# Memory attention of a streaming-encoder block: two heads' queries turned by VectorE instead of TensorE, and their attention placed one chunk later

## The chip, the cores and the metric

One core of a Trainium2 chip runs the whole layer in one launch. The metric is device time in microseconds (us); one execution was also profiled. TensorE (PE in the rows) multiplies, ScalarE (ACT) and VectorE (DVE) copy, split and normalise, GpSimd (POOL) does side work, SyncE (SP) issues the loads of the weights.

## The reference, cut to what matters

A residual stream of 256 tokens by 2048 passes an attention and convolution part, then attention over 256 memory tokens with 4 heads of 512, then a gated feed-forward part. All is float32. The change lies in the second part:

```python
def memory_cross_attention(h, mem_n, w_q_mem, w_kv_mem, w_o_mem):
    B, S, _ = h.shape
    q = (h @ w_q_mem).reshape(B, S, MEM_HEADS, MEM_HEAD_DIM)
    kv = (mem_n @ w_kv_mem).reshape(B, mem_n.shape[1], 2, MEM_HEADS, MEM_HEAD_DIM)
    k, v = kv[:, :, 0], kv[:, :, 1]
    s = jnp.einsum('bqhd,bmhd->bhqm', q, k).astype(jnp.float32) * MEM_HEAD_DIM ** -0.5
    p = jax.nn.softmax(s, axis=-1).astype(v.dtype)
    o = jnp.einsum('bhqm,bmhd->bqhd', p, v).reshape(B, S, D_MODEL)
    return o @ w_o_mem
```

## The kernel before, in words

Every weight matrix passes in 592 tiles of 128 by 1024 numbers through a ring of four slots. For tile g, SP loads `raw`; ScalarE rounds it to `w_hi` (`split_hi`, L809); VectorE stores the rest as `w_lo` (`split_lo`, L1311); TensorE multiplies with twelve matmuls (`products`, L365 to L367: lo by hi, hi by lo, hi by hi, for two token blocks and two rows of blocks). ScalarE may fill a slot again only once TensorE is through with the tile that lay in it, so each engine has a fixed order: at tile t of a chunk of eight, ScalarE and VectorE split tile t + 4, and side work stands between these splits. All orders are written by hand; each engine does its instructions in order, and a wait holds all that is behind it.

The stages around the change are the query projection (tiles from T_G, four chunks of eight tiles, chunk c giving the queries of head c) and the output projection (tiles from T_H, called H0, H1 and so on here). `acc` holds one chunk's result in two banks. At t = 7 ScalarE copies it to `stage` (`to_stage`, L1058) and so frees the banks for TensorE (`acc_free`).

A head h then goes these steps. In the kernel before they stand in chunk h + 1 (for head 3, in the output projection):

1. TensorE turns the queries, eight 128 by 128 transposes into `tp` (`turn_stage`, L377), after tile 0; ScalarE (L822) and VectorE (L1324) make `memqT` hi and lo of them.
2. Scores, 24 matmuls into `sc` (L701 to L703), after tile 2; VectorE takes the maxima (L1716, L1719), ScalarE the exponentials (L1190).
3. VectorE normalises (`m_norm`, L1722, L1725) at its t = 3, behind the split of that tile.
4. TensorE turns the probabilities (L711) after tile 5; ScalarE (L1196) and VectorE (L1730) make `probs_mT`.
5. Values, 24 matmuls (L724 to L726), after tile 6; ScalarE (L1200) and VectorE (L1735) make `oT`.

Keys (`key_h`, L1208 and L1741) and values (`val_h`, L1212 and L1745) of the next head are split at t = 5 and t = 6. For head 3 VectorE normalises before its split of that tile (H2), and TensorE turns the probabilities after H3. Chunks 1 to 3 are a loop on TensorE, ScalarE and VectorE.

Of the kernel before, what the change touches and what calls it, by code (L numbers as in the profile page):

```python
# [28 lines left out]
P = 128  # L29
# [21 lines left out]
HEAD_PE = {0: (0,), 2: (1,), 5: (3,), 6: (4,)}  # L51
HEAD_ACT = {0: (0,), 2: (1,), 5: (3,), 6: (4,)}
HEAD_DVE = {0: (0,), 2: (1,), 3: (2,), 5: (3,), 6: (4,)}


# [13 lines left out]
Q_K, Q_D, Q_F, Q_G, Q_H = 15, 19, 23, 24, 28  # L69

H_X, H_CQ, H_CKV, H_D, H_F, H_G, H_H = 0, 8, 10, 11, 19, 21, 29
# [17 lines left out]
def program(nc, x, memT, positions, vecs, w_in, w_uq, w_ukv, w_dwT, w_pw2, b_pw2, w_o, w_q_mem, w_kv_mem,  # L89
# [10 lines left out]
    with ctx:  # L100
# [142 lines left out]
        memv_ready = sem("memv_ready")  # L243
        m_scores, m_max0, m_max, m_exp, m_inv = (sem(n) for n in
# [101 lines left out]
        def _(pe):  # L346
# [342 lines left out]
            def mem_attention(t, h, q):  # L689
                if t == 0:  # L690
                    turn_stage(q, 2 * h + 2 * (S_G + 1))
                if t == 1:
                    operand_ready(q)
                    if not (isinstance(h, int) and h == 0):
                        pe.wait_ge(m_exp, 2 * h)
                    pe.wait_ge(key_lo, h + 1)
                    for b in range(NB):
                        for k in range(4):
                            o = sc[:, 0, b * TOK:(b + 1) * TOK]
                            hi, lo = (memqT[j][:, k, b * P:(b + 1) * P] for j in range(2))  # L700
                            mm(o, lo, key_h[0][:, k, :], start=k == 0, stop=False)  # L701
                            mm(o, hi, key_h[1][:, k, :], start=False, stop=False)
                            ins = mm(o, hi, key_h[0][:, k, :], start=False, stop=k == 3)  # L703
                    ins.then_inc(m_scores, 1)
                if t == 3:
                    pe.wait_ge(m_norm, 2 * h + 2)
                    if not (isinstance(h, int) and h == 0):
                        pe.wait_ge(m_out, h)
                    for kb in range(2):
                        for b in range(NB):  # L710
                            ins = turn(sc[:, 1, (2 * kb + b) * P:(2 * kb + b + 1) * P],  # L711
                                       probs_m[:, b, kb * P:(kb + 1) * P], ident[:, :])
                    ins.then_inc(m_turned, 1)
                if t == 4:
                    pe.wait_ge(m_out, h + 1)
                    if not (isinstance(h, int) and h == 0):
                        pe.wait_ge(o_done, 2 * h)
                    pe.wait_ge(val_lo, h + 1)
                    for g, bank in enumerate((ov, xt)):
                        for m in range(2):  # L720
                            for kb in range(2):
                                o = bank[:, m * TOK:(m + 1) * TOK]
                                at = slice((2 * g + m) * P, (2 * g + m + 1) * P)
                                mm(o, val_h[1][:, kb, at], probs_mT[0][:, kb, :], start=kb == 0, stop=False)  # L724
                                mm(o, val_h[0][:, kb, at], probs_mT[1][:, kb, :], start=False, stop=False)
                                ins = mm(o, val_h[0][:, kb, at], probs_mT[0][:, kb, :], start=False, stop=kb == 1)  # L726
                        ins.then_inc(m_pv, 1)
# [72 lines left out]
        def _(act):  # L800
# [251 lines left out]
            def to_stage(chunk, last_tile, fills, before, norm):  # L1052


                act.wait_ge(turned, before)
# [19 lines left out]
            for t in range(8):  # L1075
                if t == 7:
                    act.wait_ge(r_ready, R_MEM + 1)
                    to_stage(C_E, T_E + 8, 2 * S_K, 2 * (Q_B + 1), R_MEM)
# [5 lines left out]
            def key_chunk(c, second):  # L1084
                for t in range(8):
                    if t == 7:
                        to_stage(c + C_E, c * 8 + (T_E + 8), 2 * c + 2 * S_K, 2 * c + 2 * Q_K, R_MEM)
# [90 lines left out]
            def mem_attention(t, h, q):  # L1178
                if t == 0:
                    for g in range(2):  # L1180
                        if g == 0 and not (isinstance(h, int) and h == 0):
                            act.wait_ge(m_scores, h)
                        turned_hi_part(g, 2 * q + (g + 1), [memqT[0][:, 2 * g:2 * g + 2, :]])
                if t == 1:
                    act.wait_ge(m_max, h + 1)
                    if not (isinstance(h, int) and h == 0):
                        act.wait_ge(m_turned, h)
                        act.wait_ge(m_inv, h)
                    for b in range(NB):
                        fn(probs_m[:, b, :], sc[:, 0, b * TOK:(b + 1) * TOK], ACT.Exp, scale=MEM_SCALE,  # L1190
                           bias=negmax[:, b, 0:1], accum_out=rowsum[:, b, 0:1]).then_inc(m_exp, 1)
                if t == 3:
                    act.wait_ge(m_turned, h + 1)
                    if not (isinstance(h, int) and h == 0):
                        act.wait_ge(m_pv, 2 * h)
                    fn(probs_mT[0][:, :, :].rearrange("p k t -> p (k t)"), sc[:, 1, :], ACT.Copy).then_inc(m_out_hi, 1)  # L1196
                if t == 4:
                    for g, bank in enumerate((ov, xt)):
                        act.wait_ge(m_pv, 2 * h + (g + 1))
                        fn(oT[0][:, cols(h * 4 + 2 * g, 2), :].rearrange("p k t -> p (k t)"), bank[:, :], ACT.Copy)\  # L1200
                            .then_inc(o_hi, 1)

            def head_hi(t, h):

                if t == 5:
                    if not (isinstance(h, int) and h == 0):
                        act.wait_ge(m_scores, h)
                    fn(key_h[0][:, :, :], memKT[:, cols(h * 4, 4), :], ACT.Copy).then_inc(key_hi, 1)  # L1208
                if t == 6:
                    if not (isinstance(h, int) and h == 0):  # L1210
                        act.wait_ge(m_pv, 2 * h)
                    fn(val_h[0][:, :, :], memV[:, :, cols(h * CH, CH)], ACT.Copy).then_inc(val_hi, 1)  # L1212

            for t in range(8):
                if t == 7:
                    act.wait_ge(x_new, 4)
                    act.wait_ge(r_ready, R_CROSS + 1)
                    to_stage(C_G, T_G + 8, 2 * S_G, 2 * (Q_F + 1), R_CROSS)
                split_hi(T_G, t + 4)
                head_hi(t, 0)  # L1220
                if t == 1:
                    new_x_hi(3, crossT, "norm_cross", 2 * Q_F)
            with act.Fori(1, 4) as c:
                for t in range(8):
                    if t == 7:
                        to_stage(c + C_G, c * 8 + (T_G + 8), 2 * c + 2 * S_G, 2 * c + 2 * Q_G, R_CROSS)
                    split_hi(c * 8 + T_G, t + 4)
                    for step in HEAD_ACT.get(t, ()):
                        mem_attention(step, c - 1, c + (Q_G - 1))
                    head_hi(t, c)  # L1230


            for t in range(8):
                split_hi(T_H, t + 4)
                mem_attention(t, 3, Q_G + 3)
# [67 lines left out]
        def _(dve):  # L1303
# [402 lines left out]
            def mem_attention(t, h, q):  # L1706
                if t == 0:
                    for g in range(2):
                        if g == 0 and not (isinstance(h, int) and h == 0):
                            dve.wait_ge(m_scores, h)  # L1710
                        turned_lo_part(g, 2 * h + (H_G + g + 1), [[memqT[j][:, 2 * g:2 * g + 2, :]] for j in range(2)])
                if t == 1:
                    dve.wait_ge(m_scores, h + 1)
                    if not (isinstance(h, int) and h == 0):
                        dve.wait_ge(m_exp, 2 * h)
                    V.tensor_reduce(ssum[:, R_LN, :], sc[:, 0, :].rearrange("p (b k) -> p b k", b=NB), AX.X,  # L1716
                                    ALU.max, negate=True).then_inc(m_max0, 1)
                    dve.wait_ge(m_max0, h + 1)
# [337 lines left out]
```

## Time and profile before

| | |
|---|---|
| median of 3 runs | 1660.77 us (1660.75 to 1664.26) |
| the profiled execution's own time | 1661.55 us |
| its span, first to last instruction | 1659.7 us |
| granted TensorE clock, mean | 0.999 of full speed |
| TensorE busy | 1649.0 us, 99% of the span |
| VectorE, ScalarE, GpSimd busy | 68%, 50%, 7% |

The span is cut at the program's first and last instruction; the time of the execution lies 1.85 us above it. A row of the timeline gives start (us from the span's start), duration, engine, line, operation, output and inputs, shapes, and in brackets the idle time before it with what ended it. Matmuls are pipelined: one starts before the last one ended, so the distance from start to start is what one costs.

### The profile page before, as it was taken

What the parts mean: (1) busy time and instruction counts of PE and PEld (TensorE: products, weight loads), DVE (VectorE), ACT (ScalarE), POOL (GpSimd) and SP (SyncE); (2) the same over time, 40 slices, a digit from 0 to 9 for tenths busy, and PEclk for the clock granted to TensorE, in tenths of its full rate; (3) what the DMA queues carried; (4) which work ended last, traced back from release to release, by engine and by line L of the source; (5) the groups of instructions that cost most, each with busy time, mean ns of one, the idle gap of its engine ahead of it and who ended that gap; (6) DMA issues with size and microseconds to landing.
All of it is one profiled execution on the core that took longest, in us unless ns stands there. A gap on an engine that the chain in (4) does not pass through costs nothing.

```text
span 1659.7 us, 23379 instructions
## 1 busy us (share of the span) xinstructions
PE 1649.0 (99%) x7760; PEld 1379.9 (83%) x7760; DVE 1128.0 (68%) x1461; ACT 822.1 (50%) x1050; POOL 109.4 (7%) x154
## 2 busy tenths in 40 slices
PE   9999999999999999999999999999999999999997
PEld 8888888888888888888888888888888888888886
DVE  5678777778986466986568856666666666654453
ACT  7556545555546444566555544444444444344343
POOL 3100111120000000120001200000000000000000
PEclk9999999999999999999999999999999999999999
DMA  6875655556565665564446666666666666665564
GB/s 232 252 206 169 179 161 148 169 159 186 174 213 183 195 208 178 192 195 157 141 127 201 198 195 191 191 195 194 190 188 185 196 202 192 194 221 180 185 214 133
DMA packets 161114, 309.78 MB, mean 187 GB/s; under 512 B 10240, under 2 KB 16896, under 8 KB 160800
## 3 DMA queue, kind: packets, MB, share of 16 engines
q1 hardware_dynamic: 158864, 301.50, 59.1%
q0 software_dynamic: 1488, 6.42, 1.1%
q10 hardware_dynamic: 704, 1.11, 0.2%
q8 instruction: 34, 0.56, 0.1%
q14 instruction: 24, 0.20, 0.0%
HBM read 306.89 MB, written 2.10 MB: 186 GB/s over the span
## 4 chain that ended last, share of the span: by engine, by line
PE 97%; DMA 1%; ACT 1%; issue 1%; DVE 0%; SPq 0%; POOLq 0%; POOL 0%; ACTq 0%; DVEq 0%
PE acc L365 30%; PE acc L367 29%; PE acc L366 29%; PE tp L377 1%; DMA raw<-in_w_in_dram 1%; PE sc L518 1%; PE acc L594 1%; PE acc L596 1%; PE acc L595 1%; PE ov L499 0%; PE sc L513 0%; PE sc L488 0%; PE acc L565 0%; ACT w_hi L809 0%; PE acc L576 0%
## 5 line engine op out<-in xcount | busy, mean ns | idle before, releaser
L1311 DVE TENSOR_TENSOR w_lo<-raw,w_hi 128x1024 fp32r<-128x1024 f32 (+3 forms) x591 | 719.4, 1223 | 415.1 <-ACT w_hi L809 408.4
L809 ACT ACTIVATE w_hi<-raw 128x1024 fp32r<-128x1024 f32 (+3 forms) x591 | 605.7, 1027 | 752.8 <-PE acc L367 715.9
L365 PE MATMUL acc<-w_hi,crossT 128*128 128x512 f32 x832 | 324.8, 390 | 0.1
L366 PE MATMUL acc<-w_lo,crossT 128*128 128x512 f32 x832 | 323.9, 389 | 0.0
L367 PE MATMUL acc<-w_hi,crossT 128*128 128x512 f32 x832 | 323.8, 389 | 0.0
L365 PE MATMUL acc<-w_hi,mixT 128*128 128x512 f32 x732 | 289.3, 395 | 0.8 <-ACTq L904 0.6
L367 PE MATMUL acc<-w_hi,mixT 128*128 128x512 f32 x732 | 285.2, 390 | 0.0
L366 PE MATMUL acc<-w_lo,mixT 128*128 128x512 f32 x732 | 285.1, 389 | 0.0
L365 PEld LDWEIGHTS acc<-w_hi,crossT 128*128 128x128 f32 x832 | 156.2, 188 | 33.0 <-ACTq L1060 0.5
L367 PEld LDWEIGHTS acc<-w_hi,crossT 128*128 128x128 f32 x832 | 156.2, 188 | 32.7
L366 PEld LDWEIGHTS acc<-w_lo,crossT 128*128 128x128 f32 x832 | 156.3, 188 | 31.7
L365 PEld LDWEIGHTS acc<-w_hi,mixT 128*128 128x128 f32 x732 | 137.5, 188 | 30.1 <-DVE w_lo L1311 0.8
L367 PEld LDWEIGHTS acc<-w_hi,mixT 128*128 128x128 f32 x732 | 137.4, 188 | 29.2
L366 PEld LDWEIGHTS acc<-w_lo,mixT 128*128 128x128 f32 x732 | 137.6, 188 | 27.4
L365 PE MATMUL acc<-w_hi,actT 128*128 128x512 f32 x336 | 130.7, 389 | 0.0
L366 PE MATMUL acc<-w_lo,actT 128*128 128x512 f32 x336 | 130.7, 389 | 0.0
L367 PE MATMUL acc<-w_hi,actT 128*128 128x512 f32 x336 | 130.7, 389 | 0.0
L1443 DVE SCALAR_TENSOR_TENSOR conv<-uT,wdwT,conv (+1 forms) x240 | 119.1, 496 | 16.0 <-DVE conv L1443 12.5
L1800 DVE STREAM_TRANSPOSE row_bc<-stage 32x256 f32<-32x256 f32 x176 | 76.7, 436 | 3.6
L366 PEld LDWEIGHTS acc<-w_lo,actT 128*128 128x128 f32 x336 | 63.1, 188 | 13.2
L365 PEld LDWEIGHTS acc<-w_hi,actT 128*128 128x128 f32 x336 | 63.1, 188 | 13.0
L367 PEld LDWEIGHTS acc<-w_hi,actT 128*128 128x128 f32 x336 | 63.1, 188 | 13.0
(273 smaller groups left out, 1555.9 us busy)
## 6 DMA issues: line engine op xcount, KB each, us to landing
raw<-in_w_in_dram SPq DMA_DIRECT2D x104, 512.0 KB, 3.9
raw<-in_w_gate_dram SPq DMA_DIRECT2D x88, 512.0 KB, 4.2
raw<-in_w_up_dram SPq DMA_DIRECT2D x88, 512.0 KB, 3.7
raw<-in_w_down_dram SPq DMA_DIRECT2D x80, 512.0 KB, 4.7
raw<-in_w_kv_mem_dram SPq DMA_DIRECT2D x64, 512.0 KB, 3.8
raw<-in_w_o_dram SPq DMA_DIRECT2D x32, 512.0 KB, 4.4
raw<-in_w_q_mem_dram SPq DMA_DIRECT2D x32, 512.0 KB, 3.8
raw<-in_w_o_mem_dram SPq DMA_DIRECT2D x32, 512.0 KB, 3.8
```

Source lines behind the costliest of these rows:

```text
L365: mm(o, lo, whi, start=first and k == 0, stop=False)
L366: mm(o, hi, wlo, start=False, stop=False)
L367: ins = mm(o, hi, whi, start=False, stop=end)
L377: ins = turn(tp[:, bank, j * P:(j + 1) * P], src, ident[:, :])
L518: ins = mm(sc[:, h, at:at + keys], qnT[:, h, qs:qs + P], knT[:, h, 0:keys], start=False, stop=True, skip_group_check=True)
L594: mm(o, lo, w_hi[:, s, k * n:(k + 1) * n], start=first and k == 0, stop=False)
L595: mm(o, hi, w_lo[:, s, k * n:(k + 1) * n], start=False, stop=False)
L596: ins = mm(o, hi, w_hi[:, s, k * n:(k + 1) * n], start=False, stop=last and k == kt - 1)
L809: fn(w_hi[:, s, 0:width], raw[:, s, 0:width], ACT.Copy).then_inc(hi_done, 1)
L1311: V.tensor_tensor(w_lo[:, s, 0:width], raw[:, s, 0:width], w_hi[:, s, 0:width].bitcast(F32), ALU.subtract).then_inc(lo_done, 1)
L1443: ins = V.scalar_tensor_tensor(out=a, in0=u, scalar=wt, in1=a, op0=ALU.mult, op1=ALU.add)
L1800: ins = V.transpose(dst[:, :, :, 32 * i:32 * i + 32], src[:, :, :, 32 * j:32 * j + 32])
```

## The change

- The queries of heads 0 and 1 are no longer turned by TensorE. VectorE turns them in squares of 32 by 32, sixteen instructions per head from `stage` to the buffer `x_f[0]`, spread over t = 0 to 5 of chunks 1 and 2 as 3, 3, 3, 3, 2, 2; ScalarE and VectorE then make `memqT` from it at t = 6, with one instruction of 128 by 1024 each. The new semaphores are `mq_turned`, `mq_hi` and `mq_lo`.
- The attention of heads 0 and 1 moves a chunk later: scores after tile 1, probabilities after tile 4, values after tile 5 of chunks 2 and 3.
- Head 2 is still turned by TensorE, after tile 0 of chunk 3; its scores come after tile 4 there, its probabilities after tile 7, its values after tile H0.
- Head 3 keeps its places on TensorE; VectorE normalises it after the split at H2 and no longer before it.
- The splits of keys and values move with their heads. The loop over chunks 1 to 3 is written out on all three engines.

```diff
-            with pe.Fori(1, 4) as c:
+            for c in range(1, 4):
                 for t in range(8):
                     products(c * 8 + T_G, t, 8, crossT, 2 * t, 2, CH, c + C_G)
-                    for step in HEAD_PE.get(t, ()):
-                        mem_attention(step, c - 1, c + (Q_G - 1))
+                    if c == 3 and t == 0:
+                        mem_queries(2)
+                    if c > 1 and t == 1:
+                        mem_scores(c - 2)
+                    if c > 1 and t == 4:
+                        mem_probs_turn(c - 2)
+                        if c == 3:
+                            mem_scores(2)
+                    if c > 1 and t == 5:
+                        mem_values(c - 2)
+                    if c == 3 and t == 7:
+                        mem_probs_turn(2)
...
+                if t == 0:
+                    mem_queries(3)
+                    mem_values(2)
+                if t == 1:
+                    mem_scores(3)
+                if t == 3:
+                    mem_probs_turn(3)
+                if t == 4:
+                    mem_values(3)
...
+            def mem_queries_hi(h):
+
+                if h > 0:
+                    act.wait_ge(m_scores, h)
+                if h < 2:
+                    act.wait_ge(mq_turned, h + 1)
+                    fn(memqT[0][:, :, :], x_f[0], ACT.Copy).then_inc(mq_hi, 1)
...
-            with act.Fori(1, 4) as c:
+            for c in range(1, 4):
                 for t in range(8):
                     if t == 7:
-                        to_stage(c + C_G, c * 8 + (T_G + 8), 2 * c + 2 * S_G, 2 * c + 2 * Q_G, R_CROSS)
+                        to_stage(c + C_G, c * 8 + (T_G + 8), 2 * c + 2 * S_G,
+                                 *((mq_turned, c) if c < 3 else (turned, 2 * (Q_G + 1))), R_CROSS)
                     split_hi(c * 8 + T_G, t + 4)
...
+                    if c == 3 and t == 1:
+                        mem_exp(1)
+                        mem_queries_hi(2)
+                    if c == 2 and t == 1:
+                        mem_exp(0)
+                    if c > 1 and t == 2:
+                        keys_hi(c - 1)
+                    if c > 1 and t == 4:
+                        mem_probs_hi(c - 2)
+                        if c == 3:
+                            mem_exp(2)
+                    if c > 1 and t == 5:
+                        mem_out_hi(c - 2)
+                    if c < 3 and t == 6:
+                        mem_queries_hi(c - 1)
...
+            def mem_query_turns(t, h):
+
                 if t == 0:
+                    dve.wait_ge(stage_full, 2 * (S_G + h + 1))
+                    dve.wait_ge(x_lo_out, 3)
+                    if h > 0:
+                        dve.wait_ge(mq_lo, h)
+                for n in range((0, 3, 6, 9, 12, 14, 16, 16)[t], (3, 6, 9, 12, 14, 16, 16, 16)[t]):
+                    i, j = n // 4, n % 4
+                    src = stage[32 * i:32 * i + 32, :, :].rearrange("p b (k c) -> p b k c", c=P)
+                    dst = x_f[0][32 * j:32 * j + 32, :, :].rearrange("p k (b t) -> p b k t", b=NB)
+                    ins = V.transpose(dst[:, :, :, 32 * i:32 * i + 32], src[:, :, :, 32 * j:32 * j + 32])
+                if t == 5:
+                    ins.then_inc(mq_turned, 1)
...
-            with dve.Fori(1, 4) as c:
+            for c in range(1, 4):
                 for t in range(8):
                     split_lo(c * 8 + T_G, t + 4)
...
+                    if c == 3 and t == 1:
+                        mem_max(1)
+                        mem_queries_lo(2)
+                    if c == 2 and t == 1:
+                        mem_max(0)
+                    if c > 1 and t == 2:
+                        keys_lo(c - 1)
+                    if c > 1 and t == 3:
+                        mem_norm(c - 2)
+                    if c > 1 and t == 4:
+                        mem_probs_lo(c - 2)
+                        if c == 3:
+                            mem_max(2)
+                    if c < 3:
+                        mem_query_turns(t, c - 1)
+                    if c > 1 and t == 5:
+                        mem_out_lo(c - 2)
+                        if c == 3:
+                            mem_norm(2)
+                            values_lo(2)
+                    if c < 3 and t == 6:
+                        mem_queries_lo(c - 1)
...
+                if t == 0:
+                    mem_probs_lo(2)
+                    mem_queries_lo(3)
                 split_lo(T_H, t + 4)
-                if t not in (0, 2):
-                    mem_attention(t, 3, Q_G + 3)
...
+                if t == 2:
+                    mem_norm(3)
+                    values_lo(3)
```

## Rows read from the trace of the kernel before

**Rows 1.** The page: busy time of TensorE, share of the span, instructions.
```profile
PE 1649.0 (99%) x7760; PEld 1379.9 (83%) x7760; DVE 1128.0 (68%) x1461; ACT 822.1 (50%) x1050; POOL 109.4 (7%) x154
```
**Rows 2.** Timeline, chunk 1, the turn of head 0's queries among the matmuls.
```profile
752.76 0.39 PE L367 MATMUL acc<-w_hi,crossT 128*128 128x512 f32 x1
...
752.99 1.03 PE L377 MATMUL tp<-ident,stage 128*128 128x128 f32 x8
...
753.78 0.48 PE L365 MATMUL acc<-w_hi,crossT 128*128 128x512 f32 x1
...
754.10 0.40 PE L366 MATMUL acc<-w_lo,crossT 128*128 128x512 f32 x1
```
**Rows 3.** Timeline, the border from chunk 0 to chunk 1.
```profile
748.42 1.04 ACT L1212 ACTIVATE val_h<-memV 128x1024 fp32r<-128x1024 f32 x1
...
749.37 1.48 ACT L1058 ACTIVATE stage<-acc,rfac 128x512 f32<-128x512 f32 x2
749.46 0.39 PE L366 MATMUL acc<-w_lo,crossT 128*128 128x512 f32 x1
...
749.69 0.39 PE L367 MATMUL acc<-w_hi,crossT 128*128 128x512 f32 x1
...
750.13 0.19 PEld L365 LDWEIGHTS acc<-w_hi,crossT 128*128 128x128 f32 x1 [0.48 <-ACTq L1060]
750.14 0.50 PE L365 MATMUL acc<-w_hi,crossT 128*128 128x512 f32 x1
...
750.47 0.40 PE L366 MATMUL acc<-w_lo,crossT 128*128 128x512 f32 x1
```
**Rows 4.** Timeline, chunk 1, from the end of head 0's scores to its probabilities.
```profile
762.19 0.40 PE L365 MATMUL acc<-w_hi,crossT 128*128 128x512 f32 x1
...
763.12 0.17 DVE L1719 TENSOR_SCALAR negmax<-ssum 128x2 f32<-128x2 f32 x1
...
764.15 0.20 ACT L1190 ACTIVATION_READ_ACCUMULATOR probs_m<-sc,negmax 128x1 f32 x1
...
765.14 1.06 ACT L809 ACTIVATE w_hi<-raw 128x1024 fp32r<-128x1024 f32 x1 [0.79 <-PE acc L367]
...
766.23 1.23 DVE L1311 TENSOR_TENSOR w_lo<-raw,w_hi 128x1024 fp32r<-128x1024 f32 x1 [2.95 <-ACT w_hi L809]
...
767.38 0.16 DVE L1722 RECIPROCAL rowinv<-rowsum 128x2 f32<-128x2 f32 x1
...
767.57 0.62 DVE L1725 TENSOR_SCALAR probs_m<-probs_m,rowinv 128x256 f32<-128x256 f32 x2
767.66 0.39 PE L365 MATMUL acc<-w_hi,crossT 128*128 128x512 f32 x1
...
770.39 0.60 PE L711 MATMUL sc<-ident,probs_m 128*128 128x128 f32 x4
```
**Rows 5.** Timeline of VectorE, squares turned and splits close behind each other.
```profile
693.55 1.33 DVE L1670 STREAM_TRANSPOSE row_bc<-stage 32x256 f32<-32x256 f32 x3
694.90 1.23 DVE L1311 TENSOR_TENSOR w_lo<-raw,w_hi 128x1024 fp32r<-128x1024 f32 x1
```
**Rows 6.** Groups by form, VectorE, 655 to 860 us: squares; split of keys.
```profile
L1670 DVE STREAM_TRANSPOSE x_f<-stage 32x256 f32<-32x256 f32 x32 | 13.9, 435 | 0.6
...
L1741 DVE TENSOR_TENSOR row_r<-memKT,row_r 128x1024 fp32r<-128x1024 f32 x4 | 4.9, 1217 | 0.0
```
**Rows 7.** Groups by form, ScalarE, 727 to 860 us: table loads.
```profile
L809 ACT ACT_TABLE_LOAD x3 | 3.8, 1283 | 0.1
```
**Rows 8.** Timeline of ScalarE, a table load and what follows it.
```profile
37.20 1.28 ACT L891 ACT_TABLE_LOAD   x1
38.49 0.31 ACT L891 ACTIVATE trig<-resid 128x128 f32<-128x128 f32 x1
```
**Rows 9.** Timeline, output projection: head 3's normalising, the split at H2, its probabilities.
```profile
848.92 0.62 DVE L1725 TENSOR_SCALAR probs_m<-probs_m,rowinv 128x256 f32<-128x256 f32 x2
...
850.63 1.23 DVE L1311 TENSOR_TENSOR w_lo<-raw,w_hi 128x1024 fp32r<-128x1024 f32 x1 [1.09 <-ACT w_hi L809]
...
852.01 0.60 PE L711 MATMUL sc<-ident,probs_m 128*128 128x128 f32 x4
```
**Rows 10.** The page, DMA issues: KB each, median us from issue to landing.
```profile
raw<-in_w_q_mem_dram SPq DMA_DIRECT2D x32, 512.0 KB, 3.8
```

More of the change, by code:

```diff
@@ L686, in _ @@
                 x_update(c, T_F, C_F, mixT)
[L689 to L696, printed above, removed]
-                    for b in range(NB):
[L698 to L727, printed above, removed]
@@ new lines, in mem_queries, with mem_scores @@
+            def mem_queries(h):
+                turn_stage(Q_G + h - 2, 2 * (S_G + h + 1))
+            def mem_scores(h):
+                if h < 2:
+                    pe.wait_ge(mq_lo, h + 1)
+                else:
+                    operand_ready(Q_G + h - 2)
+                if h > 0:
+                    pe.wait_ge(m_exp, 2 * h)
+                pe.wait_ge(key_lo, h + 1)
+                for b in range(NB):
+                    for k in range(4):
+                        o = sc[:, 0, b * TOK:(b + 1) * TOK]
+                        hi, lo = (memqT[j][:, k, b * P:(b + 1) * P] for j in range(2))
+                        mm(o, lo, key_h[0][:, k, :], start=k == 0, stop=False)
+                        mm(o, hi, key_h[1][:, k, :], start=False, stop=False)
+                        ins = mm(o, hi, key_h[0][:, k, :], start=False, stop=k == 3)
+                ins.then_inc(m_scores, 1)
@@ new lines, in mem_probs_turn, with mem_values @@
+            def mem_probs_turn(h):
+                pe.wait_ge(m_norm, 2 * h + 2)
+                if h > 0:
+                    pe.wait_ge(m_out, h)
+                for kb in range(2):
+                    for b in range(NB):
+                        ins = turn(sc[:, 1, (2 * kb + b) * P:(2 * kb + b + 1) * P],
+                                   probs_m[:, b, kb * P:(kb + 1) * P], ident[:, :])
+                ins.then_inc(m_turned, 1)
+            def mem_values(h):
+                pe.wait_ge(m_out, h + 1)
+                if h > 0:
+                    pe.wait_ge(o_done, 2 * h)
+                pe.wait_ge(val_lo, h + 1)
+                for g, bank in enumerate((ov, xt)):
+                    for m in range(2):
+                        for kb in range(2):
+                            o = bank[:, m * TOK:(m + 1) * TOK]
+                            at = slice((2 * g + m) * P, (2 * g + m + 1) * P)
+                            mm(o, val_h[1][:, kb, at], probs_mT[0][:, kb, :], start=kb == 0, stop=False)
+                            mm(o, val_h[0][:, kb, at], probs_mT[1][:, kb, :], start=False, stop=False)
+                            ins = mm(o, val_h[0][:, kb, at], probs_mT[0][:, kb, :], start=False, stop=kb == 1)
+                    ins.then_inc(m_pv, 1)
@@ L1049, in _, with to_stage @@
             gate_and_pair(PAIRS - 1, PAIRS - 1, 1, last=True)
-            def to_stage(chunk, last_tile, fills, before, norm):
-                act.wait_ge(turned, before)
+            def to_stage(chunk, last_tile, fills, read, before, norm):
+                act.wait_ge(read, before)
                 for b in range(NB):
@@ L1175, in _ @@
                 x_update(c, T_F, 0, S_F, Z_F, R_CROSS, "norm_cross")
-            def mem_attention(t, h, q):
-                if t == 0:
-                    for g in range(2):
[L1181 to L1212, printed above, removed]
+            def mem_queries_hi(h):
+                if h > 0:
+                    act.wait_ge(m_scores, h)
+                if h < 2:
+                    act.wait_ge(mq_turned, h + 1)
+                    fn(memqT[0][:, :, :], x_f[0], ACT.Copy).then_inc(mq_hi, 1)
+                else:
+                    for g in range(2):
+                        turned_hi_part(g, 2 * (Q_G + h - 2) + (g + 1), [memqT[0][:, 2 * g:2 * g + 2, :]])
@@ new lines, in mem_exp, with mem_probs_hi @@
+            def mem_exp(h):
+                act.wait_ge(m_max, h + 1)
+                if h > 0:
+                    act.wait_ge(m_turned, h)
+                    act.wait_ge(m_inv, h)
+                for b in range(NB):
+                    fn(probs_m[:, b, :], sc[:, 0, b * TOK:(b + 1) * TOK], ACT.Exp, scale=MEM_SCALE,
+                       bias=negmax[:, b, 0:1], accum_out=rowsum[:, b, 0:1]).then_inc(m_exp, 1)
+            def mem_probs_hi(h):
+                act.wait_ge(m_turned, h + 1)
+                if h > 0:
+                    act.wait_ge(m_pv, 2 * h)
+                fn(probs_mT[0][:, :, :].rearrange("p k t -> p (k t)"), sc[:, 1, :], ACT.Copy).then_inc(m_out_hi, 1)
@@ new lines, in mem_out_hi, with keys_hi @@
+            def mem_out_hi(h):
+                for g, bank in enumerate((ov, xt)):
+                    act.wait_ge(m_pv, 2 * h + (g + 1))
+                    fn(oT[0][:, h * 4 + 2 * g:h * 4 + 2 * g + 2, :].rearrange("p k t -> p (k t)"), bank[:, :], ACT.Copy)\
+                        .then_inc(o_hi, 1)
+            def keys_hi(h):
+                if h > 0:
+                    act.wait_ge(m_scores, h)
+                fn(key_h[0][:, :, :], memKT[:, h * 4:h * 4 + 4, :], ACT.Copy).then_inc(key_hi, 1)
@@ L1214, in _, with values_hi @@
+            def values_hi(h):
+                if h > 0:
+                    act.wait_ge(m_pv, 2 * h)
+                fn(val_h[0][:, :, :], memV[:, :, h * CH:(h + 1) * CH], ACT.Copy).then_inc(val_hi, 1)
             for t in range(8):
@@ L1233, in _ @@
+                    if c < 3 and t == 6:
+                        mem_queries_hi(c - 1)
+                    if c == 3 and t == 6:
+                        keys_hi(3)
+                    if c == 2 and t == 7:
+                        values_hi(1)
+                    if c == 3 and t == 5:
+                        values_hi(2)
             for t in range(8):
+                if t == 0:
+                    mem_probs_hi(2)
                 split_hi(T_H, t + 4)
-                mem_attention(t, 3, Q_G + 3)
+                if t == 0:
+                    mem_queries_hi(3)
+                    mem_out_hi(2)
@@ L1236, in _ @@
+                if t == 1:
+                    mem_exp(3)
+                if t == 2:
+                    values_hi(3)
+                if t == 3:
+                    mem_probs_hi(3)
+                if t == 4:
+                    mem_out_hi(3)
                 if t == 7:
@@ new lines, in mem_query_turns, with mem_queries_lo @@
+                if t == 5:
+                    ins.then_inc(mq_turned, 1)
+            def mem_queries_lo(h):
+                if h < 2:
+                    dve.wait_ge(mq_hi, h + 1)
+                    V.tensor_tensor(memqT[1][:, :, :], x_f[0], memqT[0][:, :, :].bitcast(F32), ALU.subtract)\
+                        .then_inc(mq_lo, 1)
+                else:
+                    dve.wait_ge(m_scores, h)
+                    for g in range(2):
+                        turned_lo_part(g, 2 * (h - 2) + (H_G + g + 1), [[memqT[j][:, 2 * g:2 * g + 2, :]] for j in range(2)])
@@ new lines, in mem_max, with mem_norm @@
+            def mem_max(h):
+                dve.wait_ge(m_scores, h + 1)
+                if h > 0:
+                    dve.wait_ge(m_exp, 2 * h)
+                V.tensor_reduce(ssum[:, R_LN, :], sc[:, 0, :].rearrange("p (b k) -> p b k", b=NB), AX.X,
+                                ALU.max, negate=True).then_inc(m_max0, 1)
+                dve.wait_ge(m_max0, h + 1)
+                V.tensor_scalar(negmax[:, :, 0], ssum[:, R_LN, :], MEM_SCALE, None, ALU.mult).then_inc(m_max, 1)
+            def mem_norm(h):
+                dve.wait_ge(m_exp, 2 * h + 2)
+                V.reciprocal(rowinv[:, :, 0], rowsum[:, :, 0]).then_inc(m_inv, 1)
+                dve.wait_ge(m_inv, h + 1)
+                for b in range(NB):
+                    V.tensor_scalar(probs_m[:, b, :], probs_m[:, b, :], rowinv[:, b, 0:1], None, ALU.mult)\
+                        .then_inc(m_norm, 1)
@@ new lines, in mem_probs_lo, with mem_out_lo @@
+            def mem_probs_lo(h):
+                dve.wait_ge(m_out_hi, h + 1)
+                hi, lo = (probs_mT[j][:, :, :].rearrange("p k t -> p (k t)") for j in range(2))
+                V.tensor_tensor(lo, sc[:, 1, :], hi.bitcast(F32), ALU.subtract).then_inc(m_out, 1)
+            def mem_out_lo(h):
+                for g, bank in enumerate((ov, xt)):
+                    dve.wait_ge(o_hi, 2 * h + (g + 1))
+                    hi, lo = (oT[j][:, h * 4 + 2 * g:h * 4 + 2 * g + 2, :].rearrange("p k t -> p (k t)") for j in range(2))
+                    V.tensor_tensor(lo, bank[:, :], hi.bitcast(F32), ALU.subtract).then_inc(o_done, 1)
@@ new lines, in keys_lo, with values_lo @@
+            def keys_lo(h):
+                dve.wait_ge(key_hi, h + 1)
+                V.tensor_tensor(key_h[1][:, :, :], memKT[:, h * 4:h * 4 + 4, :], key_h[0][:, :, :].bitcast(F32),
+                                ALU.subtract).then_inc(key_lo, 1)
+            def values_lo(h):
+                dve.wait_ge(val_hi, h + 1)
+                V.tensor_tensor(val_h[1][:, :, :], memV[:, :, h * CH:(h + 1) * CH], val_h[0][:, :, :].bitcast(F32),
+                                ALU.subtract).then_inc(val_lo, 1)
```

86 lines of the change are left out of this document (29 added, 57 removed).

## The prediction, made before the changed kernel was run

> **What bounds the kernel now.** I read the page first: TensorE is busy for 99% of the span and runs at full clock [rows 1]. So only two things move the time: work taken from or given to TensorE, and moments in which it waits. I then read the timeline of the stage that the change touches, once for TensorE (where is the distance from one matmul's start to the next more than usual?) and once for VectorE and ScalarE (how long before TensorE needs it is each result ready?). Usual is 0.23 us for 512 columns: 749.46 to 749.69 [rows 3]. A tile of twelve is 2.72 us: two tiles lie between 762.19 and 767.66 [rows 4]. From the start of chunk 1 to the end of the output projection's first chunk, some 116 us, I find one wait over 0.1 us: 0.22 us at the border of chunks 0 and 1 [rows 3]. The reader is to see that in this stage nearly every side result is early, and that how early it is, is what the change spends.
>
> **Taken from TensorE: two turns of queries.** Without a turn the second matmul after the one at 752.76 would start 0.45 us later, at 753.21; it starts at 754.10 [rows 2]. A turn group of eight so costs 0.88 us, and two cost 1.76. Scores, probabilities and values are the same number of matmuls at other places: nothing.
>
> **Given to VectorE: 32 squares.** One takes 0.435 us [rows 6], three with a split behind them 1.34 [rows 5], thus 0.447 each and 7.15 per head. A tile has 2.72 us, a split takes 1.15 of it (766.23 to 767.38 [rows 4]). In chunk 1 three squares and a split are 2.49 us, which fits; nothing else is in VectorE's way there. The two final instructions of 128 by 1024 take the place of four of 128 by 512, on engines with time to spare. The Trainium skill (VectorE: DVE Perf Modes, Rules for kernel authors) would give a full 128 by 128 transpose to TensorE if PSUM will do as its destination; that is against this change, and by rows 2 and 5 it is right about cost (0.88 us against 7.15), but the change buys TensorE's time with VectorE's. It alters no term.
>
> **Wait 1: head 0's probabilities, in chunk 2.** Here VectorE has the squares of head 1 and the attention of head 0 together, and TensorE now turns the probabilities after tile 4, three tiles after the scores, where before it had three tiles as well but VectorE had nothing more to do. I set zero at the first matmul behind the scores (762.19 [rows 4]) and write down VectorE's queue from the same rows. Maxima end at 1.10 (763.29). The squares of t = 1 end at 2.44, under cover: the split of t = 2 can't begin before 4.04 (766.23), since it waits for TensorE's tile and for ScalarE. Then all is queue: split 1.15, keys 1.14 (1.217 less the overlap that a split shows), three squares 1.34, split of t = 3 1.15, normalising 0.81 (767.38 to 768.19). Sum 4.04 + 5.59 = 9.63, and 0.09 to reach TensorE (the copy of rows 3 ends about 750.05, TensorE goes on at 750.14). TensorE is there after three tiles, at 8.16. It waits 1.56 us.
>
> **A table load on top.** Before, ScalarE loads a function table at the top of each of the three passes of the loop [rows 7], far from anything urgent. Written out, one load is left, and I expect it directly in front of the first user, as at 37.20 [rows 8], which here is the exponential of head 0. There it costs 1.28 + 0.02 us. The exponentials end at 2.16 (764.35 [rows 4]) without it and at 3.46 with it; ScalarE's next split would begin at 2.95 (765.14). It begins 0.5 us late, the queue above has no slack behind it, and wait 1 becomes 2.06. If the load stays early or overlaps the wait for the maxima, this term is 0. The Trainium skill (ScalarE: Activation LUTs, What ACT_TABLE_LOAD costs) counts a drain of 1.38 us to every such load, 2.66 us in all; the trace has the next instruction 1.29 us after the start of the load [rows 8], so the rows show no such drain. By the rule wait 1 would be about 3.4 us.
>
> **Waits 2 and 3: normalising behind a split, one tile before its use.** Head 1 in chunk 3: VectorE's t = 3 is split, then normalising; TensorE wants it after tile 4. In the kernel before the same pair ended at 768.19, and TensorE ended the tile in question at 767.66 [rows 4]; it was not late only because the turn stood one tile further on, at 770.39. So now 768.19 + 0.09 - 767.66 = 0.62 us. Head 3: normalising was through at 849.54, before the split of H2; behind that split it ends at 850.63 + 1.15 + 0.81 = 852.59, with 0.09 for the signal 852.68, against 852.01 [rows 9]: 0.67 us. Head 2 has two tiles for it, so nothing.
>
> **Waits 4 and 5: the borders of chunks 1 to 2 and 2 to 3.** ScalarE's t = 6 is now a split and a copy of 128 by 1024 (`mem_queries_hi`) with no values between TensorE's tiles 6 and 7. That is the picture of rows 3, where `val_h` delays the emptying of `acc`: TensorE goes on at 750.14 where 749.92 was due, and the matmul after it is 0.33 behind instead of 0.23, a restart of 0.11. So 0.33 us each, 0.66. At the old two borders the values gave ScalarE time. At the border to the output projection the turn of head 2's probabilities gives it.
>
> **Priced at nothing.** The ring: a split is done 2.3 us after its slot came free (765.1 to 767.4 [rows 4]) and used three tiles, 8.2 us, after that slot came free, so 5.9 us are cover, of which the queue spends up to 2. The transfer for a slot (3.8 us [rows 10]) is issued when that split is done and is wanted when TensorE is through with the slot, 8.2 + 2.7 - 2.3 = 8.6 us later; 2 us less still cover it. Head 2's values after H0: behind tile 7 ScalarE has half of the copy to `stage` (0.74 [rows 3]), a split (0.97) and a copy of 512 columns (at most 0.74), VectorE one of 512 (at most 0.75, being half the size of a split of 1.15 with its fixed part), 3.2 us and some signals; TensorE has H0 and a turn in front of it, 3.6, and the turn of the probabilities before them. The moved splits of keys and values have a tile or more, but for the keys counted above. If the ring's cover were gone, each late microsecond would be one of TensorE's. The loop written out: branches show no gap on TensorE before; between 0 and the largest unexplained gap at a stage's edge, 0.1 us per chunk, I take 0.
>
> **Sum.** -1.76 + 1.56 + 0.50 + 0.62 + 0.67 + 0.66 = +2.25 us. Without the table term +1.75; with a restart of 0.11 after each of the three long waits +2.6. Against the profiled execution's 1661.55 that gives 1663.8; its time is 0.8 above the median of the runs, and I carry the difference to the median: 1660.77 + 2.25 = 1663.0. A measurement of this kernel can tell about 0.2%, 3.3 us, from no change: my forecast is no change that can be told.
>
> **Rivals.** A, all is covered: VectorE's queue is shorter than I write it (squares overlap with splits more, the normalising is early), the waits vanish and the turns are gained: -1.76, 1659.0. For it: the stage has hardly a wait now. Against: waits 2 and 3 need no load at all, they follow from order. Chance 0.10, with the cases between it and mine. B, the other side, slower by over 3.3 us: VectorE's queue in chunk 2 is longer, and wait 1 decides it. It needs 1.1 us more than in my sum, for instance 0.12 us more on each of the nine instructions in the queue, or a table load that holds ScalarE as long as the rule above says (there +3.6 us). Doubling wait 1 gives +4.3, 1665.1. For it: the queue has no slack, so all of it counts. Against: each duration has a row. Chance 0.14. C, writing out the loop costs instruction fetching: bounded by the parts written out before, where I find no gaps; three engines at 0.3 us per chunk would give +0.9, 1663.9. Chance 0.06, nearly all within the bound. Mine has 0.70, with 1661.8 to 1664.2 as its own range.
>
> **The range.** From 1659.5, which takes in A with half a microsecond of waits left, to 1665.3, just past B's doubled wait. Faster by over 0.2% would need -3.3 us, twice what is taken from TensorE; only the spread of the runs could show it: 0.03. Slower is B: 0.14. Same is the rest: 0.83.
>
> **What would show it.** In the changed profile: 16 transposes fewer on TensorE; VectorE gapless from the split of t = 2 to the squares of t = 3 in chunk 2; TensorE idle about 2 us before head 0's probabilities, 0.6 before those of heads 1 and 3, 0.2 at two borders; one table load in the stage, in front of head 0's exponential. Wrong would be: probabilities without a wait (A), one of over 3 us or TensorE waiting for `w_lo` (B), even thinning of matmuls (C).

## The result, and the profile after

| | before | after |
|---|---|---|
| median | 1661.20 us (20 runs) | 1663.72 us (20 runs) |
| profiled execution | 1661.55 us | 1663.47 us |
| its span | 1659.7 us | 1661.6 us |

The ratio is 1.0014, 95% interval 1.0007 to 1.0020. The changed kernel is 2.5 us slower; the interval, 1.2 to 3.3 us, leaves no doubt that it is slower, and little about the size. The forecast was +2.25 us, and no change that can be told from the spread of the times.

For differences this small the traces are sharper than the times. I take the length of the two stages that hold the change, from the first matmul of the query projection to the first of the feed-forward part, and call it the stage: 727.17 to 931.96 us before, 204.79 us; 726.75 to 933.56 us after, 206.81 us. It grew by 2.02 us. The rest of the span differs by -0.1 us net.

The page after, with the busy times, is to be read beside [rows 1]:

```profile
PE 1647.8 (99%) x7744; PEld 1378.0 (83%) x7744; DVE 1140.8 (69%) x1491; ACT 819.8 (49%) x1046; POOL 107.9 (6%) x154
```

TensorE has 16 instructions fewer and 1.2 us less of work, and yet the span is longer. So it waits, and the waits view of TensorE names for whom (us in total, times, longest; a wait is counted only from when nothing else of TensorE was in flight):

```profile
PE sc L714 <- DVE probs_m L1816: 2.5, 3, 1.5
...
PE acc L361 <- ACTq L1083: 0.5, 3, 0.2
```

Three waits for normalised probabilities, three at borders of chunks. The longest, in chunk 2, in the timelines of TensorE, VectorE and ScalarE; it is to be read beside [rows 4]:

```profile
780.47 0.40 PE L361 MATMUL acc<-w_hi,crossT 128*128 128x512 f32 x1
...
788.43 0.39 PE L363 MATMUL acc<-w_hi,crossT 128*128 128x512 f32 x1
790.32 0.55 PE L714 MATMUL sc<-ident,probs_m 128*128 128x128 f32 x3 [1.50 <-DVE probs_m L1816]
```
```profile
784.57 1.23 DVE L1379 TENSOR_TENSOR w_lo<-raw,w_hi 128x1024 fp32r<-128x1024 f32 x1 [1.64 <-ACT w_hi L832]
785.71 1.22 DVE L1835 TENSOR_TENSOR row_r<-memKT,row_r 128x1024 fp32r<-128x1024 f32 x1
786.96 1.33 DVE L1785 STREAM_TRANSPOSE x_f<-stage 32x256 f32<-32x256 f32 x3
788.31 1.23 DVE L1379 TENSOR_TENSOR w_lo<-raw,w_hi 128x1024 fp32r<-128x1024 f32 x1
789.45 0.16 DVE L1813 RECIPROCAL rowinv<-rowsum 128x2 f32<-128x2 f32 x1
789.64 0.62 DVE L1816 TENSOR_SCALAR probs_m<-probs_m,rowinv 128x256 f32<-128x256 f32 x2
```
```profile
778.93 1.28 ACT L1219 ACT_TABLE_LOAD   x1
781.60 0.48 ACT L1219 ACTIVATE probs_m<-sc,negmax 128x256 f32<-128x256 f32 x1 [1.38 <-DVE negmax L1808]
```

From 784.57 on VectorE has no idle time: split, keys, three squares, split, normalising, in this order. TensorE would have gone on at 788.66 (one matmul's 0.23 after 788.43) and goes on at 790.32: 1.66 us. The table load stands in front of the first exponential, but it runs at 778.93, while ScalarE has to wait for the maxima anyway, and is over at 780.21.

The wait before head 1's probabilities, and the border of chunks 1 and 2, to be read beside [rows 3]:

```profile
819.56 0.39 PE L363 MATMUL acc<-w_hi,crossT 128*128 128x512 f32 x1
820.43 0.66 PE L714 MATMUL sc<-ident,probs_m 128*128 128x128 f32 x4 [0.48 <-DVE probs_m L1816]
```
```profile
771.50 0.39 PE L363 MATMUL acc<-w_hi,crossT 128*128 128x512 f32 x1
772.04 0.47 PE L361 MATMUL acc<-w_hi,crossT 128*128 128x512 f32 x1 [0.15 <-ACTq L1083]
772.34 0.39 PE L362 MATMUL acc<-w_lo,crossT 128*128 128x512 f32 x1
```

Start to start is 0.87 instead of 0.23 in the first: 0.64 us lost. Head 3's (852.81 to 853.68) is the same. At the border 0.54 instead of 0.23, and 0.30 behind it: 0.39 us. The border of chunks 2 and 3 loses 0.39 too, and the old one, of chunks 0 and 1, now also 0.39 where it was 0.33. The sum is -1.76 + 1.66 + 2 x 0.64 + 2 x 0.39 + 0.06 = 2.02 us, all of the stage's growth. That it fits to the last digit is chance: other distances differ by up to 0.1 us between the two traces and cancel.

### The profile page after: what moved, and what is told of

The parts are those of the page before. It is cut to its first block, busy times and chain, and to the rows that moved or that the text cites. A ratio compares the mean times of both kernels' runs of the same rounds, so it can differ in the third digit from the quotient of the medians.

```text
span 1661.6 us, 23215 instructions
## 1 busy us (share of the span) xinstructions
PE 1647.8 (99%) x7744; PEld 1378.0 (83%) x7744; DVE 1140.8 (69%) x1491; ACT 819.8 (49%) x1046; POOL 107.9 (6%) x154
## 4 chain that ended last, share of the span: by engine, by line
PE 97%; ACT 1%; issue 1%; DVE 1%; DMA 1%; POOLq 0%; POOL 0%; ACTq 0%; SPq 0%; DVEq 0%
PE acc L361 29%; PE acc L363 29%; PE acc L362 29%; PE tp L373 1%; PE sc L514 1%; PE acc L590 1%; PE acc L592 1%; PE acc L591 1%; ACT w_hi L832 0%; PE ov L495 0%; PE sc L509 0%; DVE w_lo L1379 0%; PE sc L484 0%; DMA raw<-in_w_in_dram 0%; PE acc L561 0%
```

## The experiments

Times are compared with the kernel before run beside them; "stage" and waits come from each trace. A loss is the distance from start to start on TensorE less the usual 0.23.

**Order: normalising in front of the split.** For the three heads whose probabilities TensorE waits for.

```diff
 for t in range(8):
+    if c > 1 and t == 3:
+        mem_norm(c - 2)
     split_lo(c * 8 + T_G, t + 4)
...
-    if c > 1 and t == 3:
-        mem_norm(c - 2)
...
+    if t == 2:
+        mem_norm(3)
     split_lo(T_H, t + 4)
```

> The changed kernel, with VectorE's normalising put in front of the split of its tile again, for heads 0 and 1 (t = 3 of chunks 2 and 3) and for head 3 (H2). If order makes the waits, those before the probabilities of heads 1 and 3 (0.64 us each in the changed kernel) are gone, and the one of head 0 falls by one split, 1.15 us, from 1.66 to about 0.5. Together -2.4 us against the changed kernel, so level with the kernel before. If instead VectorE is simply too slow with the squares and its delay moves on, head 0's wait stays over 1.2 us or TensorE waits for a split instead.

Measured: 1.0005 (0.9995 to 1.0014), 1662.23 against 1661.35 us; stage 205.55 us, 1.26 less than the changed kernel's. The waits before the probabilities of heads 1 and 3 are gone and head 0's is 0.52 us, all three as expected. The sum was not: a new wait stands one tile later, before head 0's values:

```profile
789.75 1.33 DVE L1785 STREAM_TRANSPOSE x_f<-stage 32x256 f32<-32x256 f32 x3
791.10 1.22 DVE L1379 TENSOR_TENSOR w_lo<-raw,w_hi 128x1024 fp32r<-128x1024 f32 x1
792.24 0.68 DVE L1823 TENSOR_TENSOR probs_mT<-sc,probs_mT 128x512 fp32r<-128x512 f32 x1
```
```profile
791.66 0.39 PE L363 MATMUL acc<-w_hi,crossT 128*128 128x512 f32 x1
792.98 0.39 PE L729 MATMUL ov<-probs_mT,val_h 128*128 128x256 f32 x1 [0.93 <-DVE probs_mT L1823]
```

VectorE's queue simply goes on: squares, a split, then the lo part of the probabilities, at 792.24. This wait costs 1.09 us, so that only 1.26 of the 2.4 us expected are gained. Order makes the two short waits by itself; in chunk 2 order and queue work together, and whatever is next in VectorE's queue is late. The other half of the order, TensorE's turn one tile later, was not tried.

**Queue: no squares at t = 2.**

```diff
-for n in range((0, 3, 6, 9, 12, 14, 16, 16)[t], (3, 6, 9, 12, 14, 16, 16, 16)[t]):
+upto = ((0, 3, 6, 9, 12, 14, 16, 16, 16), (0, 3, 6, 6, 9, 13, 16, 16, 16))[h]
+for n in range(upto[t], upto[t + 1]):
```

> The changed kernel, with head 1's squares spread as 3, 3, 0, 3, 4, 3 over t = 0 to 5 of chunk 2 and no longer as 3, 3, 3, 3, 2, 2. If the queue of VectorE makes the wait before head 0's probabilities, it shrinks from 1.66 to 0.64 us, the same as heads 1 and 3 have, since the split of t = 3 then waits for ScalarE again: -1.0 us in all. If the three squares were counted fully it would be 0.3 us; if the squares have no part in it, it stays at 1.66.

Measured: 1.0009 (0.9999 to 1.0018), 1663.06 against 1661.35 us; stage 205.83 us, 0.98 less. VectorE is idle once more before the split of t = 3, and that sets the wait:

```profile
788.33 1.23 DVE L1379 TENSOR_TENSOR w_lo<-raw,w_hi 128x1024 fp32r<-128x1024 f32 x1 [0.36 <-ACT w_hi L832]
```
```profile
790.34 0.44 PE L714 MATMUL sc<-ident,probs_m 128*128 128x128 f32 x2 [0.48 <-DVE probs_m L1817]
```

The loss is 0.64 us, that of heads 1 and 3. So without the three squares 0.64 of the 1.66 us are left, and without the wrong order (the run before this one) 0.52. The two overlap: what each takes away, 1.02 and 1.14 us, is together more than the wait. Of the 1.34 us of squares about 1.0 counts, since VectorE would else stand idle for 0.36 us before the next split.

**Queue the other way: one and two squares more at t = 2.**

```diff
+if h == 1 and t == 2:
+    for n in (6, 7):        # one square more: (6,)
+        i, j = n // 4, n % 4
...
+        dst = junk[32 * j:32 * j + 32, 0:TOK].rearrange("p (k b t) -> p b k t", k=4, b=NB)
+        V.transpose(dst, src[:, :, :, 32 * j:32 * j + 32])
```

> The changed kernel, with two more squares on VectorE at t = 2 of chunk 2, written to a buffer that is free and not used. If VectorE's queue there has no slack, all of their 0.9 us goes into the wait before head 0's probabilities: 1.66 becomes 2.55 us, the other waits stay, and the later splits are still in time. If there is slack, less; if the ring is near its end, TensorE also waits for a split and the stage grows by more than 0.9 us.

> As more_squares, with one more square and not two: the wait before head 0's probabilities should be 1.66 + 0.45 = 2.1 us, the size that the prediction had named. After the wait of 2.56 us in more_squares TensorE's granted clock fell to the lower level for some 3.3 us and cost 1.5 us more; after 1.66 us it did not. If the fall needs a wait longer than 2.1 us, the stage is 0.45 us longer than in the changed kernel (207.3 us); if 2.1 us are enough, it is about 2 us longer.

> The kernel more_squares once more, to see whether the lower clock after its wait comes again. If it belongs to the wait, the stage is 209.2 us again and the clock falls at the same place; if it was chance, the stage is 207.7 us (the changed kernel's 206.8 and 0.9).

| | wait 1 | stage | ratio to before |
|---|---|---|---|
| changed kernel | 1.66 us | 206.81 us | 1.0014 |
| one square more | 2.11 us | 207.25 us | 1.0016 (1.0006 to 1.0026) |
| two squares more | 2.56 us | 209.23 us | 1.0024 (1.0014 to 1.0033) |
| the same again, one execution | 2.56 us | 209.15 us | 1666.30 against 1661.19 us |

Each square more lengthens the wait by 0.45 us, its own cost: no slack. But the second one lengthens the stage by 1.98 us. The windows view of TensorE (from:to, length, busy time and instructions, the granted clock as a share of full speed, DMA share, GB/s) around that wait, in the first of the two executions with two squares:

```profile
788.00:790.70 2.70, 0.36 (x2) 1.00 0.15 56
790.70:792.10 1.40, 1.34 (x7) 0.87 0.50 157
792.10:795.40 3.30, 3.30 (x10) 0.54 0.53 163
795.40:798.00 2.60, 2.60 (x23) 1.00 0.31 115
```

TensorE stands still for 2.56 us, works at full clock for about 1 us, and then its granted clock is at the lower level (1.2 of 2.4 GHz) for some 3.3 us: matmuls start 0.43 us apart instead of 0.23. That costs 1.5 us. It came in both executions profiled with this wait (the second time at 793.3, granted clock 0.55), and in no profiled execution whose wait here was 2.11 us or less. The kernel with one square more, the same stretches behind its wait:

```profile
791.70:793.10 1.40, 1.40 (x8) 1.00 0.63 176
793.10:796.40 3.30, 3.30 (x21) 1.00 0.52 158
```

That is two executions against one at 2.11 us, and the executions that were timed and not profiled speak against a clean border between 2.11 and 2.56 us. The granted clock averaged over a whole execution is 0.998 or 0.999 in all executions of all kernels but five, where it is 0.997: three of the ten with two squares more, and two of the ten with one square more. The latter two are the slowest of their ten, 1665.30 and 1665.11 us against a median of 1663.80. One execution with two squares more has 0.999 and took 1664.01 us, the shortest of its ten. A fall of 3.3 us lowers this average by 0.001, so these figures suggest, and do not show, that the clock fell in some executions at 2.11 us and not in all at 2.56 us. The medians, too, differ less than the traces: two squares more cost +3.7 us against the kernel before, the changed kernel +2.5, 1.2 us apart where the two stages are 2.4 us apart. The changed kernel at 1.66 us was at most 0.9 us of waiting away from a stall that costs more than its length.

**Borders: the copy of the queries moved behind the border.**

```diff
-                    if c < 3 and t == 6:
+                    if c < 3 and t == 7:
                         mem_queries_hi(c - 1)
...
-                    if c < 3 and t == 6:
+                    if c < 3 and t == 7:
                         mem_queries_lo(c - 1)
```

> The changed kernel, with the hi and lo of the queries of heads 0 and 1 (one 128 by 1024 instruction each on ScalarE and VectorE) moved from t = 6 to t = 7, behind the copy to stage. If that ScalarE copy makes the two new waits at the borders of chunks 1 to 2 and 2 to 3, they go (2 x 0.39 us): -0.8 us against the changed kernel, and the one of chunks 0 to 1 stays. If the borders wait for something else (the squares, which hand over stage), they stay.

Measured: 1.0009 (0.9999 to 1.0019), 1663.06 against 1661.35 us; stage 205.88 us, 0.93 less. Both new border waits are gone, the old one (0.39) stays, as expected. ScalarE is now free when the first half of `acc` is full and empties it while TensorE works on the second:

```profile
770.74 0.69 ACT L1081 ACTIVATE stage<-acc,rfac 128x512 f32<-128x512 f32 x1 [0.30 <-PE acc L363]
772.04 0.69 ACT L1081 ACTIVATE stage<-acc,rfac 128x512 f32<-128x512 f32 x1 [0.61 <-PE acc L363]
```

**What the turns are worth: sixteen transposes put back on TensorE.** Their result goes to `tp` and is not used.

```diff
+if c < 3 and t == 0:
+    pe.wait_ge(stage_full, 2 * (S_G + c))
+    for bank in range(2):
+        pe.wait_ge(turned_out[bank], Q_G)
+        for j in range(4):
+            turn(tp[:, bank, j * P:(j + 1) * P], stage[...], ident[:, :])
```

> The changed kernel, with the sixteen transposes of the queries of heads 0 and 1 put back on TensorE after tile 0 of chunks 1 and 2; their result goes to tp and is not used, the squares stay. If two turns are worth 0.88 us each, the stage is 1.76 us longer than in the changed kernel and every wait is the same length. If part of a turn was hidden before, or if the later start shortens a wait, it is less.

Measured: 1.0025 (1.0016 to 1.0034), 1665.43 against 1661.48 us; stage 208.60 us, 1.79 more, and all waits unchanged (1.66, 0.64, 0.64, and 0.39 at each border). What the change took from TensorE is gained in full.

**The table load moved away.** The changed kernel with one line more on ScalarE, `load_table(ACT.Exp)` at t = 3 of chunk 0.

> The changed kernel, with the table of the exponential loaded by ScalarE at t = 3 of chunk 0, where nothing is urgent, so that none is left at head 0's exponential. The trace of the changed kernel shows that load over before the maxima are there, so the wait before head 0's probabilities stays at 1.66 us and the stage at 206.8 us. If the load did hold back ScalarE as the prediction had it, the wait would fall by up to 0.5 us.

Measured: 1.0015 (1.0005 to 1.0025); wait 1 is 1.66 us, the stage 206.76 us. The load costs nothing where the changed kernel has it.

**The loop written out, alone**, in the kernel before.

> The kernel before, with only the loops over chunks 1 to 3 of the query projection written out on TensorE, ScalarE and VectorE. If writing out costs nothing, the time is that of the kernel before within 0.5 us and no gap appears on TensorE. If instructions are fetched more slowly, +0.5 to +1 us. Two of the three table loads on ScalarE go.

Measured: 1.0004 (0.9994 to 1.0014), 1661.87 against 1661.35 us; stage 205.22 us, 0.43 more. The times don't settle it. The one trace shows a small cost where the prediction had taken none. At the border of chunks 0 and 1 the distance is 0.54 us where [rows 3] have 0.45:

```profile
749.06 0.39 PE L367 MATMUL acc<-w_hi,crossT 128*128 128x512 f32 x1
749.60 0.47 PE L365 MATMUL acc<-w_hi,crossT 128*128 128x512 f32 x1
```

though ScalarE's copy starts 0.32 us before the first of these two matmuls in both kernels. Here the trace has the wait for the free bank as an instruction of its own, 0.05 us at 749.49, in front of the weight load; in the looped kernel the weight load itself carries that wait. That accounts for 0.06 us at the border, since the next matmul then comes 0.03 us sooner. Of the rest, some 0.15 us stands at the first value matmuls of heads 0 to 2, 0.05 each, and as much at the first score matmuls of head 3, which lie behind the loop. Why these come later, and whether they would in a second trace, is open.

**All together.** Normalising in front of the splits; head 1's squares as 4, 4, 0, 1, 3, 4; the copy behind the border; and head 0's values split at t = 4 of chunk 0.

```diff
-                if t == 6:
+                if t == 4:
                     values_hi(0)        # and values_lo(0)
...
+upto = ((0, 3, 6, 9, 12, 14, 16, 16, 16), (0, 4, 8, 8, 9, 12, 16, 16, 16))[h]
```

> All that the runs pointed to, in the changed kernel: normalising in front of the splits; head 1's squares as 4, 4, 0, 1, 3, 4 over t = 0 to 5 of chunk 2, so that neither the normalising nor the lo part of head 0's probabilities stands behind a queue; hi and lo of the queries behind the border; head 0's values split at t = 4 of chunk 0, away from the border of chunks 0 to 1. If order and queue alone made the waits, no wait over 0.1 us is left on TensorE in the stage, which is then 4.0 us shorter than in the changed kernel and 2.0 us shorter than in the kernel before (two turns, 1.76, and the old border, 0.33): 0.12% faster than before, at the edge of what can be timed. If VectorE's delay moves on once more, as it did in norm_first, a wait of 0.5 to 1 us stands before head 0's values or TensorE waits for a split.

Measured: 0.9989 (0.9980 to 0.9998), 1659.51 against 1661.48 us: faster than the kernel before by 2 us, with an interval that only just leaves out no change, and than the changed kernel by 4. Stage 202.62 us, 2.17 less than before, 4.19 less than after. All the waits counted above are gone, the old border's too. The expectation of none over 0.1 us was missed by one small delay that the kernel before has as well, at the first border inside the output projection: 907.12 to 907.49, 0.14 us late (before, 909.69 to 910.06). Where the 1.66 us stood:

```profile
787.60 0.39 PE L363 MATMUL acc<-w_hi,crossT 128*128 128x512 f32 x1
787.83 0.60 PE L714 MATMUL sc<-ident,probs_m 128*128 128x128 f32 x4
```
```profile
786.01 0.16 DVE L1814 RECIPROCAL rowinv<-rowsum 128x2 f32<-128x2 f32 x1
786.21 0.62 DVE L1817 TENSOR_SCALAR probs_m<-probs_m,rowinv 128x256 f32<-128x256 f32 x2
786.74 1.22 DVE L1379 TENSOR_TENSOR w_lo<-raw,w_hi 128x1024 fp32r<-128x1024 f32 x1
787.98 0.43 DVE L1786 STREAM_TRANSPOSE x_f<-stage 32x256 f32<-32x256 f32 x1
789.18 1.23 DVE L1379 TENSOR_TENSOR w_lo<-raw,w_hi 128x1024 fp32r<-128x1024 f32 x1 [0.76 <-ACT w_hi L832]
790.32 0.68 DVE L1824 TENSOR_TENSOR probs_mT<-sc,probs_mT 128x512 fp32r<-128x512 f32 x1
```

Normalising ends 1.0 us before it is wanted, and VectorE is idle again before the next split. Moving head 0's values away was not run alone; that it frees the old border (0.39 us) is seen only in this combination.

## Why the prediction was right

The forecast was 1663.0 us against a measured 1663.72, +2.25 us against +2.52 in the medians and +2.02 in the stage. Of the 0.72 us between the two times 0.43 lies in the median of the kernel before, 1660.77 from 3 runs and 1661.20 from 20. The mechanism was right, a gain on TensorE paid back in waits for VectorE's queue, for order and at borders. By its own steps:

| term | predicted | measured | shown by |
|---|---|---|---|
| two turns taken away | -1.76 | -1.79 | transposes put back |
| wait 1, without the table load | 1.56 | 1.66 | the trace after; no squares at t = 2, normalising in front, one square more |
| table load on top of it | 0.50 | 0 | table load moved away, and the trace after |
| wait 2 (head 1) | 0.62 | 0.64 | normalising in front |
| wait 3 (head 3) | 0.67 | 0.64 | normalising in front |
| waits 4 and 5 (borders) | 0.66 | 0.78 | copy behind the border |
| loop written out | 0 | 0.06 at the old border, 0.43 in the trace where it stands alone | loop written out, alone |

**The step that failed is the table load.** I had its place right and its time wrong. I took it to begin only when the maxima are ready, and so to make wait 1 0.50 us longer; it ran 2.7 us before the exponential, under the wait, and cost nothing. The prediction had named that case ("overlaps the wait for the maxima, this term is 0") and summed the other. The drain that the Trainium skill (ScalarE: Activation LUTs, What ACT_TABLE_LOAD costs) adds to a load is not in this trace either: in the run with the early load the load starts at 740.99 and the next instruction at 742.28. Without this term the sum would have been +1.75 us. The other terms were 0.27 us too low: 0.10 in wait 1, 0.12 at the two borders, 0.06 at the old one, less 0.01 in waits 2 and 3. So two errors of opposite sign brought 2.25 close to the stage's 2.02, and that part of the hit is luck. The time alone could not have told: +1.75 and +2.25 both lie in the measured interval.

**"Priced at nothing"** held for the ring, for head 2's values and for the moved splits: no matmul of the stage waits for `w_lo`. It held only nearly for writing out the loop.

**The rivals.** A, all is covered, did not hold for this kernel; the last experiment brings it about by order and spacing. B, a longer queue, did not come, but it was cheaper to reach than I had it: I asked for 1.1 us more of waiting, one for one. With 0.9 us more the stage of the two profiled executions is 2.4 us longer, since the clock falls; with the changed kernel's own growth that is +4.4 us, and +3.7 in the medians, past B's 3.3 either way. In the prediction this mechanism is missing altogether. C has a small part at most: the medians of the kernel with only the loops written out differ by 0.5 us from those before, within their interval.

## What to carry to other kernels

In this kernel, bound by one engine at 99%, work moved off that engine was gained in full (1.79 us for two turns), and the price was paid in how early the other engines' results are. Before moving, write down for each result how long before its use it is ready, and put the short instruction that someone waits for in front of the long one that has three tiles of time. Taking one wait away in a queue without idle time moves it to the next result in that queue; spread the new work so that the queue runs empty between two results that are wanted. A long wait of TensorE can cost more than its length: the one of 2.56 us cost 4.1 here.

## What the runs showed of the hardware that was not expected

- After TensorE had stood still for 2.56 us its granted clock fell from 2.4 to 1.2 GHz for about 3.3 us, 1 us after it had gone on, in both profiled executions; after 1.66 and 2.11 us it did not in the profiled ones. The average clocks of the executions without a profile suggest that it can fall at 2.11 us too and need not at 2.56; that was not settled.
- ScalarE's table load did not wait for what the activation behind it waits for: it starts at 778.93, the exponential at 781.60, once the maxima are there.
- With the loop written out a matmul that waits at a chunk's border starts 0.09 us later than in the loop, with the same work around it (0.54 against 0.45 us); the wait is then an instruction of its own on TensorE.
